# Starting an output projection beside the last step of an RWKV mixer

## The reference, cut to what matters

```python
out_b, v_l = rwkv7_mixer(pb, vres, ...)              # 384 of the 1024 mixed columns
...
x = x + jnp.concatenate([out_a, out_b, out_m], axis=-1) @ w_out[l]
x = x + conv_ffn(rms_norm_2(x, ffn_norm_g[l]), w_up[l], conv_w[l], conv_b[l], w_down[l])
```

## Time and profile before

| | us |
|---|---|
| median of 3 runs | 3563.51 |
| the profiled execution, its own time | 3567.69 |
| its span in the trace | 3565.8 |
| TensorE busy | 3389.7 (95% of the span) |
| VectorE / ScalarE / GpSimd busy | 1474.7 / 1051.3 / 338.4 |
| mixer's last `finish`, from its first state product to the projection's first matmul | 2697.0 to 2730.8 |

### The profile page before, as it was taken

How to read it: one execution, slowest core, us unless ns; L and a number is a source line. 1 busy time by engine, 2 the same in 40 slices (tenths; PEclk the granted TensorE clock), 3 DMA queues, 4 the chain that set the end, 5 groups by cost and what they waited for, 6 DMA issues and landing times. The chain is left out here.

```text
span 3565.8 us, 37968 instructions
## 1 busy us (share of the span) xinstructions
PE 3389.7 (95%) x16472; PEld 2563.3 (72%) x16472; DVE 1474.7 (41%) x2049; ACT 1051.3 (29%) x1515; POOL 338.4 (9%) x322
## 2 busy tenths in 40 slices
PE   6999999989899999999998989999998999999999
PEld 3445556666667888888886766788886888888887
DVE  5245434566443211113337342455643443333333
ACT  4222222443332211112115553333323322222211
POOL 1000002333213000000003000021221100000000
PEclk9999999999999999999999999899998999999999
DMA  5111110000013111112122010000003111111211
GB/s 231 41 59 48 60 60 15 24 12 12 13 71 136 53 48 48 48 42 85 47 76 86 24 37 28 7 1 1 1 1 133 56 48 48 48 48 36 101 43 70
DMA packets 35254, 182.29 MB, mean 51 GB/s; under 512 B 4261, under 2 KB 4261, under 8 KB 21648
## 3 DMA queue, kind: packets, MB, share of 16 engines
q1 hardware_dynamic: 22176, 133.18, 10.5%
q0 software_dynamic: 12912, 46.69, 3.4%
HBM read 161.89 MB, written 17.96 MB: 50 GB/s over the span
## 5 line engine op out<-in xcount | busy, mean ns | idle before, releaser
L525 PE MATMUL ps<-r,r 128*128 128x512 f32 x2656 | 1056.7, 398 | 14.4 <-DVE r L1988 13.1
L527 PE MATMUL ps<-r,r 128*128 128x512 f32 x2656 | 1048.0, 395 | 0.0
L526 PE MATMUL ps<-r,r 128*128 128x512 f32 x2656 | 1047.9, 395 | 0.0
L525 PEld LDWEIGHTS ps<-r,r 128*128 128x128 f32 x2656 | 501.4, 189 | 142.3 <-issue 20.8
L526 PEld LDWEIGHTS ps<-r,r 128*128 128x128 f32 x2656 | 501.6, 189 | 117.2 <-issue 3.2
L527 PEld LDWEIGHTS ps<-r,r 128*128 128x128 f32 x2656 | 501.3, 189 | 115.7
L515 PE MATMUL ps<-ar 128*128 128x128 f32 (+7 forms) x2228 | 448.1, 358 | 7.0 <-DVE ar L1992 3.3
L515 PEld LDWEIGHTS ps<-ar 128*128 128x128 f32 (+3 forms) x2228 | 274.6, 177 | 166.1 <-issue 139.8
L1394 ACT ACTIVATE ar<-ps 128x512 f32<-128x512 f32 (+3 forms) x336 | 173.2, 540 | 719.5 <-PE ps L627 169.9
L1981 DVE TENSOR_TENSOR r<-ar,r 128x1024 fp32r<-128x1024 f32 (+1 forms) x170 | 204.6, 1204 | 325.0 <-ACT r L1356 324.9
L1356 ACT ACTIVATE r<-ar 128x1024 fp32r<-128x1024 f32 (+1 forms) x170 | 174.4, 1033 | 551.8 <-PE ps L527 510.9
(11 more groups left out here) (274 smaller groups left out, 3291.7 us busy)
## 6 DMA issues: line engine op xcount, KB each, us to landing
ar<-in_w_mod SPq DMA_DIRECT2D x24, 1024.0 KB, 4.9
ar<-in_w_gu SPq DMA_DIRECT2D x22, 1024.0 KB, 4.9
ar<-in_w_up SPq DMA_DIRECT2D x22, 1024.0 KB, 4.8
ar<-in_w_in SPq DMA_DIRECT2D x19, 1024.0 KB, 4.9
ar<-in_w_dn SPq DMA_DIRECT2D x32, 512.0 KB, 3.5
x<-ar POOLq DMA_DIRECT2D x48, 256.0 KB, 2.3
ar<-x POOLq DMA_DIRECT2D x24, 512.0 KB, 7.3
ar<-in_xT POOLq DMA_DIRECT2D x16, 512.0 KB, 14.0
```

Of the source, the lines that this page charges most:

```text
L525: M.matmul(o, whk, hi[k][:, a:a + n], start=k == 0, stop=False)
L526: M.matmul(o, whk, lo_[k][:, a:a + n], start=False, stop=False)
L527: ins = M.matmul(o, wlk, hi[k][:, a:a + n], start=False, stop=k == nk - 1)
```

## The change

Three blocks of the projection (`AHEAD = 3`, m = 0, 1, 2 on the first 512 tokens) are now issued on TensorE by `first_blocks`, laced four matmuls at a time with the rounds of `finish(5)`. Their weights are rounded and split there too. Fifteen of the sixteen input roundings (`EARLY`; all but tile 5 on the last 512 tokens, which the last step itself writes) are laced into the groups of step 5 on ScalarE and on VectorE. The homes of the first three weight blocks are exchanged: blocks 0 and 1 use homes 1 and 2, whose former contents are dead by then, and block 2 uses home 0, which is free only after the readout of step 5. GpSimd reloads the residual as soon as step 4 has been mixed and the masks of step 5 are applied.

```diff
@@ -241,17 +241,19 @@
         split_before[name] = in_home.get(home)
         in_home[home] = name
 
+    HOME_OF = {1: range(7), 2: (1, 2, 0, 3, 4, 5, 6)}
+
     def fetch_ffn(tag, w_out, w_gu, w_dn):
         for i in range(4):
             fetch(("wo", tag, i), w_out[i])
             for j in range(2):
                 split(("wo", tag, 2 * i + j), ("wo", tag, i), 1024 * j,
-                      home=("out", 2 * i + j) if 2 * i + j < 7 else turn_of_home[0])
+                      home=("out", HOME_OF[tag][2 * i + j]) if 2 * i + j < 7 else turn_of_home[0])
         turn_of_home[0] = 1 - turn_of_home[0]
         for m in range(22):
             fetch(("gu", tag, m), w_gu[m])
             for j in range(2):
-                split(("gu", tag, m, j), ("gu", tag, m), 1024 * j, home=("out", 0) if m == 1 and j == 0 else None)
+                split(("gu", tag, m, j), ("gu", tag, m), 1024 * j, home=("out", HOME_OF[tag][0]) if m == 1 and j == 0 else None)
         for part in range(3):
             for m in range(8):
                 fetch(("dn", tag, part, m), w_dn[part][m])
@@ -392,6 +394,10 @@
 
     STEPS = range(6)
     lam = math.exp(-0.5)
+
+
+    EARLY = [(k, a) for a in (0, 512) for k in (1, 2, 0, 6, 3, 4, 7)] + [(5, 0)]
+    AHEAD = 3
     r8 = Region(FT, H2)
     raw_tiles = [r8.tile(1024) for _ in range(10)]
     raw = [raw_tiles[n_] for n_ in (0, 1, 2, 3, 4, 5, 6, 8, 7, 9)]
@@ -854,7 +860,7 @@
 
         def out_projection(tag):
             for a in (0, 512):
-                for m in range(8):
+                for m in range(AHEAD if tag == 2 and a == 0 else 0, 8):
                     name = ("wo", tag, m)
                     key = (*name, a)
                     pe.wait_ge(*v_lo.at(("w", name)))
@@ -1319,10 +1325,31 @@
                 yield
                 yield
 
+            def first_blocks():
+
+                yield
+                for m in range(AHEAD):
+                    name = ("wo", 2, m)
+                    key = (*name, 0)
+                    pe.wait_ge(*v_lo.at(("w", name)))
+                    o = claim(key, m, (v_res, key))
+                    wh_, wl_ = homes[split_home[name]]
+                    n_ = 0
+                    for k in range(8):
+                        if m == 0:
+                            pe.wait_ge(*v_lo.at((("mix", 2), (k, 0))))
+                        for w_, x in ((wh_, hhi), (wh_, mlo), (wl_, hhi)):
+                            ins = M.matmul(o, w_[:, k * 128:k * 128 + 128], x[k][:, 0:512], start=n_ == 0, stop=n_ == 23)
+                            n_ += 1
+                            if n_ % 4 == 0 and n_ < 24:
+                                yield
+                    ins.then_inc(*product(key))
+                    yield
+
             together(prepare(0), raws(range(5, 10), (0, 1, 3)))
             for s in STEPS:
                 together(group(s, 0), group(s, 1), *([prepare(s + 1)] if s < 5 else []), *([finish(s - 1)] if s else []))
-            together(finish(5))
+            together(finish(5), first_blocks())
             stage_done(pe, ("pe", "rwkv", 0))
 
         start_and_norm()
@@ -1617,13 +1644,8 @@
 
         def out_projection(tag, shift):
             if tag == 2:
-                split(("wo", 2, 0))
-                for a in (0, 512):
-                    for k in range(8):
-                        mixed(2, k, a)
-                    if a == 0:
-                        split(("wo", 2, 1))
-            for m in range(2, 8):
+                mixed(2, 5, 512)
+            for m in range(2 if tag == 1 else AHEAD, 8):
                 split(("wo", tag, m))
             split(("gu", tag, 0, 0))
             for a in (0, 512):
@@ -1944,10 +1966,29 @@
                 A.activation(e1_f, e1_f, ACT.Exp, scale=-0.5).then_inc(*a_rstd(("rs", "ry", s)))
                 yield
 
+            def rounded_early():
+                for k, a in EARLY:
+                    if (k, a) == (7, 0):
+                        for j in range(2):
+                            act.wait_ge(*product.at(("rk", (5, j))))
+                    if (k, a) == (5, 0):
+                        act.wait_ge(*v_step.at(("mix", 4)))
+                    mixed(2, k, a)
+                    yield
+
+            def first_blocks():
+                split(("wo", 2, 0))
+                split(("wo", 2, 1))
+                for _ in range(9):
+                    yield
+                act.wait_ge(*product.at(("ry", 5)))
+                split(("wo", 2, 2))
+
             together(prepare(0), raws(range(5, 10)))
             for s in STEPS:
-                together(group(s, 0), group(s, 1), *([prepare(s + 1)] if s < 5 else []), *([finish(s - 1)] if s else []))
-            together(finish(5))
+                together(group(s, 0), group(s, 1), *([prepare(s + 1)] if s < 5 else [rounded_early()]),
+                         *([finish(s - 1)] if s else []))
+            together(finish(5), first_blocks())
             stage_done(act, ("act", "rwkv", 0))
 
         start_and_norm()
@@ -2328,16 +2369,14 @@
                         low_h(tag, k - 1, a, shift)
 
             if tag == 2:
-                split(("wo", 2, 0))
-                for a in (0, 512):
-                    for k in range(8):
-                        mixed(2, k, a)
-                    if a == 0:
-                        split(("wo", 2, 1))
+                split(("wo", 2, 3))
+                mixed(2, 5, 512)
             for a in (0, 512):
                 for m in range(8):
-                    if a == 0 and 0 < m < 7:
-                        split(("wo", tag, m + 1))
+                    if a == 0 and tag == 1 and 0 < m < 7:
+                        split(("wo", 1, m + 1))
+                    if a == 0 and tag == 2 and m < 4:
+                        split(("wo", 2, m + 4))
                     if a == 0 and m == 7:
                         split(("gu", tag, 0, 0))
                     if a == 0:
@@ -2743,10 +2782,27 @@
                 dve.wait_ge(*v_step.last())
                 V.tensor_tensor(bonus, y_f, ggs[s % 3], ALU.mult).then_inc(*v_step(("mix", s)))
 
+            def rounded_early():
+                yield
+                for k, a in EARLY:
+                    mixed(2, k, a)
+                    yield
+
+            def first_blocks():
+                yield
+                split(("wo", 2, 0))
+                yield
+                yield
+                split(("wo", 2, 1))
+                for _ in range(8):
+                    yield
+                split(("wo", 2, 2))
+
             together(prepare(0), raws(range(5, 10)))
             for s in STEPS:
-                together(group(s, 0), group(s, 1), *([prepare(s + 1)] if s < 5 else []), *([finish(s - 1)] if s else []))
-            together(finish(5))
+                together(group(s, 0), group(s, 1), *([prepare(s + 1)] if s < 5 else [rounded_early()]),
+                         *([finish(s - 1)] if s else []))
+            together(finish(5), first_blocks())
             stage_done(dve, ("dve", "rwkv", 0))
 
         start_and_norm()
@@ -2888,7 +2944,9 @@
                     else:
                         pool.wait_ge(*product.at(("y", (s, j), Lv // 2)))
                     G.tensor_tensor(th(AM), th(AT), bc4(M_UP[Lv]), ALU.mult).then_inc(*p_mask(("am", (s, j), Lv)))
-        stage_over(pool, "rwkv", 0)
+        for j in range(2):
+            pool.wait_ge(*v_evac.at(("rk", (5, j))))
+        pool.wait_ge(*v_step.at(("mix", 4)))
         for k in range(8):
             for a in (0, 512):
                 pool.wait_ge(*tile_out[k][a // 512].at(("x2", k, a)))
```

## The result

The changed kernel takes 3555.19 us (median of 11 runs, 3550.30 to 3560.03), the kernel before 3563.44 in the same session (median of 11). The ratio is 0.9976, with a 95% interval of 0.9967 to 0.9985: a gain of 8.25 us. The forecast was 17.5 us: the direction came, and a little less than half of the size.

A forecast was written before the change was run, and what follows sets the result against it. TensorE, busy 95% of the span, was taken as the bound. Block 3 starting at 2731.9 instead of 2749.37 saves 17.5 us (about 8 from lower clock, the rest waits), so 3563.51 becomes 3546.0 us; 8-in-10 range 3542 to 3554.

The forecast's parts named there:

- Step 5: Fifteen early input roundings on ScalarE and VectorE would make this step 1.0 us longer, bounds 0 and 19.4 us.
- the slow rival: Roundings add pauses that drop the clock in step 5; kernel slower once its delay passes 18.5 us, 3580 us; chance 0.03.
- Both ways meet: Before block 3: TensorE's early matmuls end at 2731.9, mixing, rounding and split at 2731.8; block 3 starts 17.5 us earlier.
- the length of the half clock: Early rounds before the readout: clock falls near 2702, about 3.4 us at half clock, costing 1.7 us.
- the 8.0 of this step: First early matmul to readout at full clock: 28 projection matmuls 6.35 us plus five state products 1.65 us.
- the weights come late: Block 0's first weight fetch lands late with 7 MB moving at once; costs up to 5.2 us, 3551.2 us; chance 0.10.
- the rival with half clock in the readout: Clock still at half in step 5's readout; costs 11 us, leaving 6.5 us gain, 3557 us; chance 0.09.

The follow-up runs named there:

- h3_roundings_only: Changed kernel without the three early blocks (`AHEAD = 0`); the early roundings and early reload stay. 3565.37 us, ratio 1.0007 to the kernel before.
- first profile: The profiled execution of the changed kernel that the result came with, ahead of the follow-up runs; 3555.02 us by its own time.
- g1_split3_early: Changed kernel with block 3's weights split ahead of `stage_done` instead of behind it. 3551.00 us, ratio 0.9966 to the kernel before.
- g2_control: Also called the control: the changed kernel run again, unaltered, beside the other experiments. 3554.43 us, ratio 0.9974 to the kernel before.
- h2_filler: Changed kernel plus six unread constant matmuls in TensorE's two pauses at the start of `finish(5)`. 3553.16 us, ratio 0.9973 to the kernel before.
- h1_reload_late: Changed kernel with GpSimd's reload of x held until block 0's weight has landed. 3555.35 us, ratio 0.9976 to the kernel before.

## Why the prediction was wrong

**What held.** The blocks fill the waits, the clock is full in the readout (7.6 us, forecast 7.4) and in both sums, and the wait of 8.20 is gone. The wait for the first state update is 1.76 where it was 1.04, or 0.72 more, where 0.65 was forecast, and the wait for the sum of step 4 is 2.21 where it was 1.69. Without the blocks the kernel is not faster (`h3_roundings_only`).

**Step 5.** I took 1.0 us for it. It cost 0.5 in the first profile and 1.9 to 2.0 in the six others, where the clock fell for some 3 us behind the wait of 2.21. So the slow rival, the roundings that take the clock out of step 5, came in a small form: step 5 lost 2.0 us in all, where the rival needed 18.5 to make the kernel slower. The wait of 2.21 is the same in all seven, so it does not by itself explain the fall, and why the first profile has none stays open.

**What failed: "Both ways meet".** This step took ScalarE to start its rounding and split right behind the mixing, at 2728.7 plus the handoffs. It missed that `stage_done` makes ScalarE and VectorE wait for TensorE's last early matmul. The two ways therefore do not meet, they stand in series: TensorE's 36 matmuls, then rounding, split, low part, 3.12 us, and half clock for 3 us behind it (9 matmuls in 3.67, 2733.87 to 2737.54, where 9 x 0.227 is 2.0: 1.6). That is 4.7 us, the largest part. `g1_split3_early` removes it and gets 3.4 to 4.4. The code of `stage_done` showed the dependence before any run.

**What was mis-sized: the length of the half clock.** The step had a fall near 2702 for 3.4 us at 1.7. The fall came, 2.4 us after T0 in the control instead of 4.0, and lasted some 10 us, at a cost of 3.5 (`h2_filler` against the control): 1.8 more. The 3.4 came from the earlier trace rows, where TensorE had a run of small products behind one pause. The mixture here, four wide matmuls and a state product in turn, is a case that the trace of before did not have. Beside it stands a smaller term: at full clock a group of four takes 1.12, not 0.91, between two small products (1.38 a turn in `h2_filler`, forecast 1.24), so the 8.0 of this step is 9.15 without any fall: 1.1 more.

**What was a rival: the weights come late.** I gave it 0.10 and took the contention as 0. In the first profile the split waits 9.61 for the DMA until 2695.15 and the first early matmul comes 1.2 late; the fetch needs 10.7 to the split where I reckoned 8.1. In the control it is 9.0 and costs nothing, and without the reload in its way 6.0, still nothing (`h1_reload_late`). So it is a cost of some executions, 1.3 us in the first profile against the control.

**The sum.** From T0 to the fourth block 7.7 us are missing: 1.2 (weights), 3.1 (from the first early matmul to the readout: 12.8 for 9.7), 3.3 (of it 3.12 the new wait). Behind it 2.9 are missing: 1.6 of half clock, and 1.3 that I did not foresee, of which the next row is 0.83:

```profile
2809.30 0.47 PE L531 MATMUL ps<-r,r 128*128 128x512 f32 x1 [0.83 <-issue]
```

TensorE waited there for nothing that the profile shows, near the change from the first to the second half of the tokens. The row is in every profile with the early blocks and in neither of those without. Its cause is not settled: the place of the instructions in the program is a guess, and I ran nothing that tells it apart. The remaining 0.5 is not traced. Of the 10.6 missing in all, step 5 gives 0.5 back. In the control 9.1 are missing from T0, with no late weights among them, and step 5 adds 1.0: from S to the end it is 10.1 in both.

**What brings the clock back.** Between the forecast and the rival with half clock in the readout stood one question: whether seven rounds of wide matmuls bring the clock back. Being busy was not enough for the readout's own products: in the kernel before they ran at 0.50 with TensorE busy for 13.87 of 15 us, and in `h3_roundings_only` for 13.96 of 15. With the early rounds ahead of it the clock was back at 1.00 by 2706.8, and the same readout ran at 1.00, as I forecast. What I had no row for is how long that takes. That the lacing with small products is what made it some 10 us is not shown, since even dense matmuls took 3 us once and 6 us another time.

## What to carry to other kernels

When work is put beside the end of a stage, look first at what closes the stage: a mark that makes the other engines wait for the last thing recorded turns "beside" into "behind", and the code of that wait shows it before a run. A pause costs twice where the clock falls behind it (here 3.12 us, and 1.6 more at half clock); take the length of a fall from a place with the same mixture of work, or bound it from both sides. Measure small gains from a mark ahead of all that the change touches, since the part before it moved by 8.3 us between profiles (S stands at 2623.56 in `h1_reload_late` and at 2631.85 in `h2_filler`), more than most of the edits here were worth. A mark inside the change hides what lies ahead of it: from T0 the control looks 1.5 us better than the first profile, and from S they are equal.

## What the runs showed of the hardware

Full and half clock are the granted clock at 1.00 and 0.50.

- With TensorE busy for 8.98 of 9.50 us on groups of four 128x512 matmuls and a 64x64 state product in turn (the first profile after), the clock was at 0.50, and full again by 2706.8. It had fallen behind a pause of 1.76 us: in the control it was at 0.50 from the end of the next state product, before the second pause. With filler products in both pauses, idle 0.27 us once, it stayed at 1.00 (`h2_filler`).
- Behind a wait of 2.21 us in step 5 the clock fell to 0.50 for some 3 us in six of seven profiles; behind 1.69 us at the same place in the kernel before it stayed at 1.00.
- After a pause of 3.12 us, dense 128x512 matmuls ran at half clock for 3 us in the control and 6 us in `h2_filler`, the same instructions behind the same wait. Why the lengths differ is open.
- A 128x512 matmul in a group of four between small products takes 0.28 us at full clock; in a dense row of 36 it takes 0.24, in the projection 0.227 (`h2_filler`, and the earlier trace rows).
- An engine held its stream behind an instruction that waited: ScalarE's split of block 3 started at 2731.33, behind a rounding that had waited 5.46 us, and at 2725.74 in `g1_split3_early`, where it stands ahead of that rounding.
- A fetch of 1 MB, with more weights behind it in SP's queue, took 6.0 us to its first use (`h1_reload_late`), and beside a reload of 4 MB on GpSimd's queue 9.0 (`g2_control`) to 10.7 (the first profile after).
